# An even layer's index products and choice of keys moved beside the later weight products, and two attention passes joined into one of 16 units

## The reference, cut to what matters

```python
def _even_mixer(h, w_in, ...):
    aq, ak, av, bq, bk, bv, iq, ik, iw = _split_cols(h @ w_in, EVEN_SIZES)
    aq = _rms_norm(aq.reshape(b, s, A_HEADS, 2, HEAD_DIM), qn_a)      # 4 heads of 2 x 64
    ak = _rms_norm(ak.reshape(b, s, A_HEADS, 2, HEAD_DIM), kn_a)
    ya = _diff_attention(aq, ak, av, lam, _alibi_slopes(A_HEADS))     # p0 - lam * p1, times av
    ya = _rms_norm(ya, subln_a) * (1.0 - lam_init)
    bq = _rms_norm(bq.reshape(b, s, B_HEADS, HEAD_DIM), qn_b)         # 8 heads of 64
    bk = _rms_norm(bk, kn_b)
    iw = iw * IDX_HEADS ** -0.5
    yb = _dsa_attention(bq, bk, bv, iq, ik, iw, _alibi_slopes(B_HEADS), 64)
    return concatenate([ya, yb])                                      # then y @ w_out
# inside _dsa_attention, for each block of 128 queries:
    idx_logits = einsum('bqhd,bsd->bqhs', iqi, ik) * IDX_DIM ** -0.5  # 8 index heads
    score = einsum('bqhs,bqh->bqs', relu(idx_logits), iwi)
    score = where(causal, score, -inf)
    _, sel = top_k(score, 64)                                         # keys for the softmax
```

## Time and profile before

| | |
|---|---|
| median of 3 runs | 1421.41 us (1421.3 to 1422.6) |
| the profiled execution's own time | 1419.48 us |
| its span on the core | 1417.8 us |
| mean granted TensorE clock | 0.894 of 2.4 GHz |
| PE busy | 1169.2 us (82%) |
| DVE busy | 631.1 us (45%) |
| ACT busy | 483.1 us (34%) |
| DMA | 368.65 MB, mean 260 GB/s |
| first product of the even layer | at 669.3 us |
| first scores of attention 2 | at 747.9 us |
| last scores of attention 3 | at 842.4 us |
| transposes of `hn` for the output product | at 855.3 us |

### The profile page before, as it was taken

The page is one execution under the profiler, slowest core; times in us unless marked ns, Lnnn a source line. Parts: engine busy times, 40 slices in busy tenths (PEclk is TensorE's granted clock), DMA queues, the critical chain, the costliest instruction groups (busy, mean ns, idle before and its releaser), DMA issues.

```text
span 1417.8 us, 19477 instructions
## 1 busy us (share of the span) xinstructions
PE 1169.2 (82%) x7659; PEld 857.0 (60%) x7659; DVE 631.1 (45%) x1281; ACT 483.1 (34%) x783; POOL 7.6 (1%) x54
## 2 busy tenths in 40 slices
PE   7889878667576675766997788999999998999998
PEld 6665665234232341323774448899997646999986
DVE  5745552001001010003844576765545676775543
ACT  5544511000000000003623245554434456565441
POOL 1000000000000000000000000000000000000000
PEclk9997879889887898878997569999999989999999
DMA  8635459999999999999465332856455680855420
GB/s 304 239 122 189 182 220 411 428 431 430 429 429 429 430 429 431 428 420 386 151 224 191 119 120 88 270 178 239 178 208 179 234 300 2 282 181 188 183 90 30
DMA packets 121775, 368.65 MB, mean 260 GB/s; under 512 B 9890, under 2 KB 56141, under 8 KB 110926
## 3 DMA queue, kind: packets, MB, share of 16 engines
q1 hardware_dynamic: 120604, 367.26, 67.5%
q10 hardware_dynamic: 1074, 0.08, 0.1%
HBM read 366.28 MB, written 1.05 MB: 259 GB/s over the span
## 4 chain that ended last, share of the span: by engine, by line
PE 53%; DMA 22%; DVE 16%; ACT 5%; issue 3%; SPq 1%; DVEq 0%; ACTq 0%
PE ps L1925 51%; DMA more<-in_w_up_dram 8%; DMA more<-in_w_down_dram 6%; DMA more<-in_w_gate_dram 6%; DVE ring_r L33 3%; PE ps L1929 3%; DVE st L33 3%; DVE R_c L33 2%; DVE X_c L33 1%; DVE R_c_r L33 1%; DMA ring<-in_ada_w_dram 1%; DVE sc L33 1%; DVE R_a L33 1%; SPq L688 1%; DVE x L33 1%
## 5 line engine op out<-in xcount | busy, mean ns | idle before, releaser
L1925 PE MATMUL ps<-ring,xg 128*32 128x512 f32 x640 | 139.7, 734 | 126.3 <-DMA more<-in_w_gate_dram 78.5
L1925 PE MATMUL ps<-hT_r,ring_r 128*128 128x256 f32 x800 | 224.6, 281 | 0.0
L1925 PEld LDWEIGHTS ps<-ring,xg 128*32 128x32 f32 x640 | 36.8, 132 | 222.1 <-issue 222.1
L1925 PE MATMUL ps<-R_c_r,W_c_r 128*128 128x256 f32 (+1 forms) x624 | 154.5, 284 | 0.0
L33 DVE TENSOR_TENSOR ring_r<-ring,W_c_r 128x1024 fp32r<-128x1024 f32 x94 | 115.2, 1225 | 86.9 <-ACT W_c_r L33 82.4
L1925 PEld LDWEIGHTS ps<-hT_r,ring_r 128*128 128x128 f32 x800 | 152.4, 191 | 0.0
L1925 PE MATMUL ps<-R_c_r,X_c_r 128*128 128x256 f32 (+1 forms) x624 | 151.0, 283 | 0.6 <-DVE R_c_r L33 0.4
L33 DVE TENSOR_TENSOR ring_r<-ring,X_c_r 128x1024 fp32r<-128x1024 f32 x88 | 107.8, 1225 | 86.8 <-ACT X_c_r L33 83.5
L1925 PE MATMUL ps<-more,xg 128*32 128x512 f32 x384 | 134.2, 721 | 0.0
L33 ACT ACTIVATE W_c_r<-ring 128x1024 fp32r<-128x1024 f32 x94 | 99.6, 1060 | 75.9 <-PE ps L1925 70.4
L33 DVE TENSOR_TENSOR x<-x,ps 128x512 f32<-128x512 f32 x36 | 24.8, 688 | 218.4 <-PE ps L1925 218.1
(11 more groups left out here) (293 smaller groups left out, 1916.7 us busy)
## 6 DMA issues: line engine op xcount, KB each, us to landing
ring<-in_ada_w_dram SPq DMA_DIRECT2D x24, 2048.0 KB, 8.4
ring<-in_w_gate_dram SPq DMA_DIRECT2D x20, 2048.0 KB, 16.6
ring<-in_w_up_dram SPq DMA_DIRECT2D x20, 2048.0 KB, 18.6
ring<-in_w_down_dram SPq DMA_DIRECT2D x20, 2048.0 KB, 17.6
more<-in_w_gate_dram SPq DMA_DIRECT2D x12, 2048.0 KB, 26.5
more<-in_w_up_dram SPq DMA_DIRECT2D x12, 2048.0 KB, 27.5
more<-in_w_down_dram SPq DMA_DIRECT2D x12, 2048.0 KB, 26.5
ring<-in_ffn_gate_dram SPq DMA_DIRECT2D x22, 1024.0 KB, 5.5
```

The source lines that it names most:

```text
L1925: return pe.matmul(out, lhsT, rhs, start=start, stop=stop, skip_group_check=True)
```

## The change

Product order. It was `ak`, `aq`, `av`, `kvi`, `tli`, `bq`; it is `kvi`, `tli`, `ak`, `aq`, `bq`, `av`. Side work of the even layer stands in `Lanes`, in which every generator advances one step at each call. The index products run in banks 4 and 5 in place of bank 7. `sco` and `wrk` move to the free halves of `hn`, one pair for each query block; `rel` becomes two buffers inside `kvi` and `tli`. Attentions 2 and 3 become one line of 16 units with an ada row at each even unit, and the loads of the output weights behind the row of unit 10. For the four heads with `lam`, DVE's three instructions of `norms` become two, and the copy out of bank 6 goes from DVE to ACT, which scales it. In `headnorm` the two halves of the squares get buffers of their own, here and in the other layers. Loads of ada rows that are used among products give their slot back before the load ahead of them in the ring's order.

```diff
+class Lanes:
+    def go(self, n=1):
+        for g in list(self.work):
+            try:
+                next(g)
+            except StopIteration:
+                self.work.remove(g)
...
+    p.product("tli", 2)
+    p.product("ak", 4)
+    p.close(("f", len(p.chunks) - 3))
+    p.ada(("f", len(p.chunks) - 1))
+    for name in ("aq", "bq", "av"):
         p.product(name, 4)
...
-    p.units(2, 8, (0, 2, 4, 6))
-    p.units(3, 8, (0, 2, 4, 6), 2, 1)
+    p.units(2, 16, (0, 2, 4, 6, 8, 10, 12, 14), 10, 1)
...
-            order.append(z)
+            order.insert(len(order) - (k in ahead), z)
...
-        sco, wrk, rel = R1c[:, 6144:6400], R1c[:, 6400:6656], R1c[:, 6656:7168]
+        sco, wrk = [hn[:, a, 512:768] for a in range(2)], [hn[:, a, 768:1024] for a in range(2)]
+        rel = [kvi[:, :, 128:384], tli]
...
             def headnorm(src, n):
                 m = 2 if n <= 4 else 1
+                if s_hred.name in C.n:
+                    act.wait_ge(*C.now(s_hred))
                 for a in range(0, 2, m):
-                    if s_hred.name in C.n:
-                        act.wait_ge(*C.now(s_hred))
-                    q = sc[:, 0:64 * n * m].rearrange("p (a h d) -> p a h d", a=m, d=64)
+                    q = sc[:, 512 * a:512 * a + 64 * n * m].rearrange("p (a h d) -> p a h d", a=m, d=64)
...
+                    if unit.lam is not None:
+                        act.wait_ge(s_pv, at_n.pv[u])
+                        copy(mix[:, unit.a, 128 * unit.dst:128 * unit.dst + 128], ps[6][:, 0:128], scale=s4[:, U % 8, 4:5], up=s_fin)
...
+            def work_tli():
+                yield from steps(2)
+                pe.wait_ge(s_ik, 1)
+                headturn(tli[:, :, 56:184], 1, [6])
+                headturn(ikd, 1, [7])
+                yield from steps(2)
+                for a in range(2):
+                    w = 128 * (a + 1)
+                    for hp in range(4):
+                        take(4, 5)
+                        pe.wait_ge(s_hv, 8)
+                        for i in range(2):
+                            mm(ps[4 + i][:, 0:w], iqT[64 * i:64 * i + 64, hp, 128 * a:128 * a + 128],
+                               ikT[64 * i:64 * i + 64, 0, 0:w], True, True).then_inc(s_ix, 1)
+                        free[4] = free[5] = C.next(s_rl)
+                        yield
...
-            side.until(ev, "qk")
-            attend(2, 2, {0: [(s_hv, 8), (s_ev, 16), (s_lam, 1)]})
-            side.add(steps(5))
-            side.until(ev, "sel0", "bT")
-            attend(3, 2, {0: [(s_hv, 15), (s_ev, 18)]})
-            side.end()
+            attend(2, 2, {0: [(s_hv, 13), (s_lam, 1)], 2: [(s_ev, 22)], 8: [(s_hv, 15)]})
```

More of the change, by code:

```diff
@@ L75, in until, with __init__, add, end @@
             self.go(1)
+class Lanes:
+    def __init__(self):
+        self.work = []
+    def add(self, g):
+        self.work.append(g)
+    def go(self, n=1):
[4 more added lines that the diff above has]
+                self.work.remove(g)
+    def end(self):
+        while self.work:
+            self.go()
+    def until(self, ev, *names):
+        while any(n not in ev for n in names):
+            self.go()
 class Feed:
@@ L207, in make_plan @@
                 p.experts.append(p.load("moe", name, g, q))
-    k = p.load("w", "ak")
-    p.first["ak"] = len(p.chunks)
+    k = p.load("w", "kvi")
+    p.first["kvi"] = len(p.chunks)
     for q in range(3):
@@ L388, in build @@
         last_in = {}
+        ahead = {plan.ada_order[v][2] for point, row in plan.rows.items() for v, what in row if what == "run" and point[0] in "nf"}
         for k in range(nload):
@@ L740, in gpsimd @@
             G = Chain(pool, s_pool)
-            side = Side()
-            steps = lambda n: iter(range(n))
             G(pool.memset, ident[:, :], 0.0)
@@ L759, in gpsimd @@
             G(pool.iota, iotI[:, :], pattern=[[1, 32]], base=0, channel_multiplier=0, up=s_iota)
-            def attend(n, beside):
-                for u in range(len(attns[n].units)):
-                    side.go(beside)
-                    if n == 3 and u == 4:
-                        side.until(ev, "sel1")
             G(pool.memset, zero[:, :], 0.0)
@@ L877, in scores @@
                     side.go(beside)
-                    if n == 3 and u == 4:
-                        side.until(ev, "sel1")
+                    lanes.go()
                     ada(("u", n, u))
@@ L1102, in work_bq, with lane, then @@
-            def work_bq():
-                yield from headnorm(heads(bq), 8)
-                ev.add("bT")
-                yield
-                yield from indexer(0)
-                yield from indexer(1)
-            feed.then[first["ak"] + 3] = ends("ak", ak, [0, 1], work_ak())
-            for i in range(first["ak"], first["ak"] + 4):
-                if i == first["ak"] + 2:
+            def lane(name, dst, bs, work):
+                def then():
+                    evacuate(dst, bs, first[name] + (1 if name == "tli" else 3))
+                    lanes.add(work)
+                return then
@@ new lines, in scalar @@
+            feed = Feed(lambda i: begin(i, XFc), lanes, lag=5)
+            for q in range(2):
+                feed.ahead(first["kvi"] + q)
+            def work_tli():
+                yield from steps(4)
+                for a in range(2):
+                    w = 128 * (a + 1)
+                    for hp in range(4):
+                        n = 4 * a + hp
+                        act.wait_ge(s_ix, 2 * n + 2)
+                        if n >= 2:
+                            act.wait_ge(s_iw, n - 1)
+                        for i in range(2):
+                            S(act_op, rel[n % 2][:, i, 0:w], ps[4 + i][:, 0:w], ACT.Relu, up=s_rl if i else None)
+                        yield
@@ L1116, in scalar @@
-            feed.product(first["kvi"], 4, ends("kvi", kvi, [0, 1], headnorm(heads(kvp[:, :, 0:64]), 1)))
-            feed.product(first["tli"], 2, ends("tli", tli, [2, 3], steps(3)))
-            feed.product(first["bq"], 4, ends("bq", bq, [4, 5], work_bq()))
-            feed.drain()
-            side.until(ev, "qk")
-            attend(2, 2)
-            def work_sub():
-                yield from head_norm128()
-                yield from steps(2)
-            side.add(work_sub())
-            side.until(ev, "sel0", "bT")
@@ L1319, in scores @@
                 def scores(u):
+                    if u in work:
+                        side.add(work[u]())
                     side.go(beside)
-                    if n == 3 and u == 4:
-                        side.until(ev, "sel1")
+                    lanes.go()
+                    if n == 2 and u in (8, 12):
+                        lanes.until(ev, f"sel{u // 4 - 2}")
                     ada(("u", n, u))
@@ L1713, in vector @@
                     overflow()
-            feed = Feed(lambda i: begin(i, XFc), side, lag=5)
-            scattered(NX // 4 - 1, {3: lambda: [feed.ahead(first["ak"] + q) for q in range(2)]})
-            def work_ak():
-                yield from headnorm(heads(ak), 8, st[:, 128:144], 1.0)
-            def work_aq():
-                headturn(akT, 4, g_ka, [6, 7])
+            lane = lambda work: lambda: lanes.add(work)
+            feed = Feed(lambda i: begin(i, XFc), lanes, lag=5)
+            scattered(NX // 4 - 1, {3: lambda: [feed.ahead(first["kvi"] + q) for q in range(2)]})
@@ L1761, in indexer, with top64 @@
+                headturn(bkT, 1, g_kb, [7])
+            def top64(a, later):
+                w = 128 * (a + 1)
+                w_ = wrk[a][:, 0:w]
+                cur = sco[a][:, 0:w]
+                yield from steps(1 + later)
                 dve.wait_ge(s_as, a + 1)
```

283 lines of the change are left out of this document (107 added, 176 removed).

## The result

| | before | changed |
|---|---|---|
| median | 1421.54 us (4 runs, 1421.3 to 1422.6) | 1382.66 us (4 runs, 1379.21 to 1386.69) |
| the profiled execution | 1419.48 us, span 1417.8 | 1382.33 us, span 1380.6 |
| mean granted clock | 0.894 | 0.906 |
| DVE busy in the span | 631.1 us | 625.9 us |

What follows compares the result with a forecast made beforehand. PE was taken as held up by side work and a low clock. The attention, 42.6 + 3.7 + 3.0 + 3.0 + 12.9 = 65.2 us, taken as 65, gives 42.4; with products, 43.4 off 1421.41: 1378.0 us, range 1368 to 1400.

Steps and rivals of the forecast that it cites:

- Products: Even layer's weight products, now with the index steps: net -1 us, bounds -3 and +6.
- 4.5 us of idle time: Weight products: 4.5 us of the stage's 6.2 us of idle PE taken as removed.
- the term of 1.5 us for the slower clock: Weight products: 1.5 us saved on about eight slow products behind the 2.51 us wait.
- Start: Between units 1 and 2 PE turns `bq` in about 1.3 us, where it stood 5 us before.
- Units: Attention to last scores: 42.6 us PE work, plus 3.7 for doubled DVE rounds, 3.0 sub-norm, 3.0 clock.
- Tail: From the last scores to the transposes of `hn`: the same chain remains, 12.9 us.
- The 3.0 us for the sub-norm: Units 13 to 15: DVE's sub-norm beside unit work adds 3.0 us before the last scores.
- Clock: Attention: one drop of about 6 us at half speed allowed, +3.0 us.
- The rival of the low clock: Attention: granted clock stays at 0.64, stage 78 us, total 1391 us; chance 0.15.
- DVE as the bound: Attention: PE ends each unit waiting for DVE, stage about 73 us, total 1386 us; chance 0.12.
- Loads: Attention's ada and output-weight loads: costed at nothing; rival of late loads 73 us or more, 1388 us, chance 0.05.
- The edits costed at nothing: Swapped ada load slots, separate buffers for squares, shortened `norms` and the copy given to ACT: no gain counted.

Runs made afterwards that it cites:

- the repeat: The changed kernel run once more without an edit: 1382.59 us (1379.31 to 1386.02, 5 runs).
- the kernel with the broken line: The changed kernel with its 16 units in two lines of 8, draining behind unit 7: 1388.38 us, ratio 0.9746.

## Why the prediction came out as it did

*Products: -1 forecast, +1.3 and +2.9 measured in two profiles.* The index products and DVE's load were right: 61.9 us busy for "some 60", and the first scores were not late. The 4.5 us of idle time were right too in the first profile: PE stood idle 6.2 us of the stage before and 1.7 after (2.6 in the repeat), the new wait included. What failed is the busy time: PE was to be busy 3.3 us more (4.8 for the index products less 1.5 for the clock) and is 5.4 more, 6.0 in the repeat. So the step that failed is the term of 1.5 us for the slower clock; the other 0.6 us were not placed. The drop behind the wait of 2.51 us is gone, but a new wait of 1.65 to 2.62 us stands where the first ada row is closed, with a drop of its own:

```profile
697.00:700.00 3.00, 3.00 (x9) 2.33 (x8) 2.71 (x3) 0.00 (x0) 0.00 (x0) 0.50 1.07 404
```

```profile
681.00:683.00 2.00, 2.00 (x6) 1.60 (x5) 1.90 (x2) 1.51 (x2) 0.00 (x0) 0.50 0.00 0
```

The first row is the kernel before, the second the changed one; the drop is some 3.5 us long in both. Nine profiles have this closing and the new slot order. PE waits there in all of them, 1.61 to 2.62 us, and their products fall into three lengths: 78.25 us in the one with no drop behind the wait, 79.8 in three with the short drop, 81.4 in five with one of some 7 us. This close moved from 37.5 us behind the layer's first product to 10 us behind it, where ACT's copy is not done. The prediction looked at products and transposes and not at the closings. Moving the close only moved the wait. Its bounds, -3 to +6, held.

*Start.* Right: `bq` is turned in 1.09 us with a wait of 0.15 in place of 4.96.

*Units.* Forecast 42.6 + 3.7 + 3.0 + 3.0 to the last scores, 52.3; measured 49.8. The parts agree less than the sum. PE's idle time there is 6.1 us, for 3.7 and 3.0 of waits behind DVE. Its busy time of 43.7 us contains two drops of the clock, 8.9 us of work in the first and third of the windows above; at the 1.92 for 3.64 us of an ada row they cost about 4 us (an estimate), for 3.0. That leaves some 39.5 us of work at full clock, where the sum had 42.6. About half of the difference has a place: the sum took off 3.1 us for what is missing at both ends of the line (2.4 and 0.7), while in the trace the value products of five units and the transposes of three, 4.5 to 5 us by their lengths in the earlier trace rows, come behind the last scores. The rest was not placed. The 3.7 us that leaving the rounds out saves match the term in part by luck, since 1.0 of them is clock, which the sum had in another term, and one round of the eight was left in.

*Tail.* 12.9 us forecast as the same chain, 16.2 measured. It was PE's clock and DVE's load that changed: DVE is busy 10.5 us in it, and was 7.9 before.

```profile
842.42:855.27 12.85, 7.82 (x61) 5.33 (x61) 7.87 (x20) 8.85 (x21) 0.00 (x0) 0.82 0.01 1
```

The 3.0 us for the sub-norm may thus have come at least in part behind the last scores and not before them. How much of the 3.3 us is the sub-norm was not tried.

*Clock.* One drop of 6 us was allowed and three came, 20 us in all with the last in the tail. PE was busy 4.0 of 4, 4.9 of 6 and 6.5 of 10 us in them, so the last one costs least where it stands. What it costs shows behind it, in 29 PE instructions where there could be 48. "The output product keeps its slow start" was right.

*Sum.* 41.4 us measured for 42.4 in the attention; the median, 1382.66 us, is 4.7 us above the 1378.0 forecast. The mechanism was right and the agreement is luck in part: units 2.5 us shorter than forecast and a tail 3.3 us longer nearly cancel. The rival of the low clock foresaw 0.64 throughout; the units have 0.90. DVE as the bound foresaw 73 us. Loads never made PE wait in the units, although the DMA share rose from 0.36 to 0.82.

*The edits costed at nothing.* The squares: right. The shorter `norms` and the copy given to ACT: no run takes them back, so their price is not known. The slot order: the sentence "PE is full there, so nothing either" was wrong as a price. Without the swap the same change would have gained some 33 us and not 39.

*The odd layer.* No step had it, and it is the largest part of the miss in the profile: 3.5 us. Over the fourteen profiles its attention took 64.7 and 64.95 us in the kernel before, and in the twelve with the change 64.4 three times, 67.2 to 67.3 seven times and 68.1 to 68.2 twice, with the same instructions. What differs is where the half clock falls, and with it PE's waits. In the three short ones among the twelve the clock is low in one piece of some 13.5 us behind a wait of 2.65 us near the start. In the changed kernel it is low for 3.4 us there and comes back, PE then waits 1.25, 0.95 and 2.31 us for DVE where the short ones have one wait of 0.84 us or so, and the clock falls again on later work. The short one (rounds left out), then the changed kernel:

```profile
1090.00:1103.00 13.00, 11.91 (x54) 4.92 (x54) 10.13 (x38) 5.04 (x16) 0.00 (x0) 0.50 0.91 354
```

```profile
1098.00:1107.00 9.00, 5.65 (x46) 2.92 (x42) 7.47 (x32) 4.26 (x13) 0.00 (x0) 1.00 0.90 327
1108.69 1.11 PE L1898 MATMUL ps<-ident,R_c 128*128 128x128 f32 x4 [2.31 <-DVE R_c L33]
```

So full clock where DVE leads won nothing: it ended in a wait. The higher value comes without the new slot order (67.25 us) and without the new buffers (68.2), so it needs neither, and three kernels with the change have the lower one. Whether it makes the higher value likelier than it was (none of two before, nine of twelve after) stays open.

## What to carry to other kernels

When generators or products change their order, list everything that hangs on a chunk's number, the closings of side rows and the release of ring slots too: here the products missed their forecast by 2.3 us with one new wait at such a closing, and one slot line was worth 6. Spread a burst of DVE work over as many pipeline steps as its deadline allows; leaving out two rounds to a unit took 3.7 us off the units, and giving them one to a unit took 2.6 us off units and tail, with a median 5.8 us lower. When an edit is to remove a wait, check in the trace that it touches the unit whose wait it is: the second bank here went to units 13 and 15, and the waits stood before 11 and 12. When a sum over a pipeline comes out, check its parts: here two of them missed by 2.5 and 3.3 us with opposite signs.

## What the runs showed of the hardware

Waits of PE of 0.8 to 2.6 us were followed in most profiles by 3 us or more at 1.2 GHz (3 to 10 us in the changed kernel's units and tail, up to 14 in the units of others), on work that began when the wait was over or 2 us behind it. The drop did not always come: at the first closing the kernel with spread rounds waited 1.61 us and kept 1.00, where the changed kernel waited 1.65 and fell; with the closing one chunk later a wait of 3.01 us had no drop behind it; and before the row of unit 14 both the changed kernel and the one with spread rounds waited 1.24 us, the first keeping 1.00 (1.92 us for the row) and the second falling (3.42 us). So the length of a wait did not say here whether the clock would fall. The Trainium skill, "TensorE: Matmul & The Clock Gate", section "HAM oscillation — how this bites in real kernels", describes such swings behind waits for DMA; in this trace they stand behind short waits for ACT and DVE. With transposes without a use between the groups of the tail, the tail's clock was 0.79 in one kernel and 0.99 in the other, for 0.67 without, and both began the output product at 1.00.

Because the drops fall differently each time, the same code took 64.4 to 68.2 us in the odd attention and 78.25 to 81.4 in the products, and single executions of the changed kernel differ by up to 7.5 us (nine executions), of the kernel with the broken line by 13.2. A median of five does not tell edits of 2 us apart here; the length of the edited stretch in a profile often does, if its clock row is read with it.
